# A two-layer diffusion step on one core: modulation products placed singly between filter transform products, gate rows moved inside the transform and ahead of the last row tile

## The chip, the cores and the metric

The kernel runs on one core of one Trainium2 chip. The metric is the device time of one execution in microseconds (us); smaller is better.

## The reference

Two layers work on 1024 sample tokens and 128 prompt tokens of width 1024, all in 32-bit floats. The attention groups and the output projection are untouched by the change. What matters here is the opening of a layer:

```python
mod = silu(c) @ ada_w[i] + ada_b[i]              # (1, 3072), for sample and for context
shift, scale, gate = split(mod, 3)
h = rmsnorm(x, norm_pre) * (1 + scale) + shift
out = mixer(h)                                   # one input projection, four mixers, one output projection
x = x + gate * rmsnorm(out, norm_post)
# one mixer is a Hyena long convolution of order 2: its two filters come from a small
# network times a decay, and are applied through a Fourier transform
spec = rfft(u, 2n) * rfft(filt, 2n); y = irfft(spec)[:n]
```

## The kernel before

The program is written engine by engine. Each engine runs its own list in order; semaphores tie them together. There is no planner: the order in the source is the order on the engine. Token rows are held as nine tiles of 128 (eight of the sample, one of the prompt). All matmul results go to the eight banks of PSUM. `K.next()` hands banks out in turn, so a job takes the bank that the job eight turns earlier had; `claim` makes TensorE wait until that earlier user has been read out (`emptied`), and `done`/`full` tell the reader that a bank is filled.

A layer opens as follows. For filter `o` = 1 and then 0, TensorE makes the nine tiles of the filter (`f3`), which VectorE multiplies by the decay and folds. Then it makes the transform `FE`: turns 0 to 3 (`FE_ORDER`), each with two jobs `p`, and after turn 1 the prompt's job `FEp`. A job of turns 0 and 1 has 4 products of 256 columns, one of turns 2 and 3 has 8, `FEp` has 2. Every 32-bit product shows in the trace as two matmul records and two weight loads, so turns 0 and 1 with `FEp` are 36 records, and turns 2 and 3 are 64.

Six blocks `ada(j)` of the modulation row (silu of the conditioning times a block of 512 columns) stand between these. ScalarE copies each out of its bank (`take_ada`), GpSimd adds the bias (`bias_ada`) and signals `ada_biased`. Block 5 belongs to the gate. In the second filter's transform (`o` = 0):

- TensorE waits for `ada_biased` 3, and turns shift and scale into columns: 16 products (job `modT`), each with a whole 128x128 weight load and only 2 columns. They stand in one block ahead of turn 0. After turn 1 come `FEp` and `ada(5)`, then turns 2 and 3, then the wait for `ada_biased` 5 and the four gate products of 512 columns (`gate_row`), then the transposes of the normalised rows (`x_turned`, L670) and the first input projection, `hyena_input(0, 0)`.
- ScalarE starts on this transform only when the first filter's butterfly and spectrum are finished, since they share buffers. It empties three `FE` banks, then goes on in turns: square of row tile 0, `FE`, square of tile 1, `FEp` (L1381), `take_ada(5)` (L1332), and then again an `FE` bank (L1371) and a square (L1341), up to tile 5.
- VectorE first finishes the butterfly of filter 1 (its last instruction is L1910), and then reads `modT` (L1826, L1827), which frees its bank. It normalises row tiles 0 to 5 (L1772, and L1844 when GpSimd has made the root), multiplies the four gate rows by a norm's gain (`gate_rows`), adds the filter bias (L1897), and then modulates the transposes with ScalarE: VectorE does half of each tile (L1852), ScalarE the other (L1390). `hyena_input(0, 0)` waits until row tiles 0 to 3 are modulated in both halves.
- GpSimd makes the inverse roots of tiles 0 and 1, then `bias_ada(5)`, then the roots of tiles 2 to 5.
- SyncE issues the loads. It stores the gate rows once they are read out of their banks, and loads row tiles 6 to 8 behind that.

Of the kernel before, what the change touches and what calls it, by code (L numbers as in the profile page):

```python
# [37 lines left out]
P = 128  # L38
D = 1024
KD = D // P  # L40
# [95 lines left out]
RING = len(XN)  # L136
# [148 lines left out]
class Banks:  # L285
# [25 lines left out]
    def claim(self, job, banks, drains=1):  # L311

        found = {self.last[b] for b in banks if b in self.last}
        b0 = banks[0]
        self.filled[b0] = self.filled.get(b0, 0) + 1
        self.drains[b0] = self.drains.get(b0, 0) + drains
        for b in banks:
            self.last[b] = (b0, self.drains[b0])
        job = (self.s.layer, job)
        assert job not in self.jobs, job  # L320
        self.jobs[job] = (b0, self.filled[b0], self.drains[b0])
        return [(self.s.raw(f"bank{b}_drained"), v) for b, v in sorted(found)]
# [26 lines left out]
def program(nc, I, outs, known=None):  # L349
    with ExitStack() as ctx:  # L350
        ctx.enter_context(nc.allow_non_contiguous_dma(reason="a few short parameter columns"))
        S = Signals(nc, ctx, known)
        K = Banks(S, known)
# [27 lines left out]
        def at(off, *shape, parts=P, base=0):  # L381

            v = R[base:base + parts, off:off + int(np.prod(shape))]
            if len(shape) == 1:
                return v
            g = "abcd"[:len(shape)]
            return v.rearrange(f"p ({' '.join(g)}) -> p {' '.join(g)}", **dict(zip(g, shape)))

        ident = sb("ident", [P, P])
        sel = sb("sel", [P, 2, P])  # L390
# [268 lines left out]
        def _(pe):  # L659
            def claim(job, banks, drains=1):  # L660
                for w in K.claim(job, banks, drains):
                    pe.wait_ge(*w)
                return bank[banks[0]]

            def mm(out, lhsT, rhs, start=True, stop=True):
                return nc.tensor.matmul(out, lhsT, rhs, start=start, stop=stop)  # L666
# [24 lines left out]
            for l in S.layers():  # L691
# [19 lines left out]


                mod = at(A_MOD, 3072)
                tf = at(TF, 2 * NT, 2, P)
                ti = at(TI, 2 * NT, 2, P)
                eo = at(EO, TT, 3, GW)
                for o in (1, 0):
                    for t in FILTER_ORDER:
                        ps = claim(("f3", o, t), K.next())
                        for h, row0, c, n in (((0, 0, 512, 64), (1, 64, 0, 64)) if t == 4 else  # L720
                                              ((t // 5, 0, t * P - t // 5 * HALF, P),)):
                            last = mm(ps[row0:row0 + n, :], at(F_ARG + c, n, parts=64, base=64 * h),
                                      at(A_FW3 + o * 512, 512, parts=64, base=64 * h))
                        last.then_inc(*K.done(("f3", o, t)))
                    ada(0 if o else 4)
                    if o:
                        pe.wait_ge(*S.at("transform_table"))
                    else:
                        if l == 0:
                            pe.wait_ge(S.raw("constants"), 16 * N_CONST)  # L730
                        pe.wait_ge(*S.at("ada_biased", 3))
                        ps = claim(("modT",), K.next())
                        for m in range(2 * KD):
                            last = mm(ps[:, 2 * m:2 * m + 2], mod[:, m * P:(m + 1) * P], sel[:, :, 0])
                        last.then_inc(*K.done(("modT",)))

                    for turn, a0 in enumerate(FE_ORDER):
                        back = (4 - a0) % 4
                        if a0 % 2:
                            pe.wait_ge(*K.emptied(("f3", o, 7)))  # L740
                            pe.wait_ge(*S.at("filter_negated", o))
                        else:
                            pe.wait_ge(*S.at("filter_folded", (o, a0 + 4)))
                        if o and turn % 2:
                            ada((turn + 1) // 2)
                        if o == 0 and turn == 2:
                            ada(5)
                        for p in range(2):
                            ps = claim(("FE", o, a0, p), K.next())
                            for ri in range(2):  # L750
                                if a0 % 2:
                                    terms = [(a, 0) for a in (a0, a0 + 4)] + [(a, 1 + ri) for a in (back, back + 4)]
                                else:
                                    terms = [(a, 2 * ri) for a in (a0, a0 + 4)]
                                for i, (a, kind) in enumerate(terms):
                                    last = mm(ps[:, ri * GW:(ri + 1) * GW], tf[:, 2 * a + p, ri, :],
                                              eo[:, a, kind, :], i == 0, i == len(terms) - 1)
                            last.then_inc(*K.done(("FE", o, a0, p)))
                        if turn == 1:
                            pe.wait_ge(*S.at("filter_folded", (o, NT)))  # L760
                            ps = claim(("FEp", o), K.next())
                            for ri in range(2):
                                last = mm(ps[:, ri * GW:(ri + 1) * GW], tf[:, 0, ri, :], eo[:, NT, 2 * ri, :])
                            last.then_inc(*K.done(("FEp", o)))
                    if o:
                        ada(3)
                    else:
                        pe.wait_ge(*S.at("ada_biased", 5))
                        for s in range(2):
                            for half in range(2):  # L770
                                ps = claim(("gate_row", s, half), K.next())
                                mm(ps[:, :], sel[:, s, :], mod[:, 2 * D + half * 512:2 * D + (half + 1) * 512]
                                   ).then_inc(*K.done(("gate_row", s, half)))

                def x_turned(t, banks):
                    pe.wait_ge(*S.at("x_normed", t))
# [93 lines left out]
                for o in range(2):  # L870
                    for a0 in (0, 2, 1, 3):
# [4 lines left out]
                        for p in range(2):  # L876
                            ps = claim(("Z", o, a0, p), K.next())
                            for ri in range(2):
                                for i, a in enumerate((a0, a0 + 4)):
                                    last = mm(ps[:, ri * GW:(ri + 1) * GW], tf[:, 2 * a + p, ri, :],  # L880
                                              zv[:, a, 2, :], i == 0, i == 1)
# [368 lines left out]
                for grp in ("gqa", "diff0", "diff1"):  # L1250
# [3 lines left out]
                    for i in range(1, TT + 1):  # L1254
# [3 lines left out]
                        t = i + AHEAD[grp] - 1  # L1258
# [501 lines left out]
        def _(v):  # L1760
# [49 lines left out]
            for l in S.layers():  # L1810
# [20 lines left out]
                def gate_rows():  # L1831

                    for s in range(2):
                        for half in range(2):
                            job = ("gate_row", s, half)
                            v.wait_ge(*K.full(job))
                            tt(at(SGH + s * D + half * 512, 512), B(job), at(A_NPOST + half * 512, 512), ALU.mult
                               ).then_inc(*K.drained(job))
# [45 lines left out]
                for o in (1, 0):  # L1884
                    if o == 0:
                        modulation()
                        for t in range(RING):
                            normalize(t)
                        gate_rows()

                    for a0 in range(4):
                        for p in range(2):
                            v.wait_ge(*K.emptied(("FE", o, a0, p)))
                    E = at(B2, 4, 2, 2, GW)
                    bias = at(A_HBIAS[o], GW)
                    for p in range(2):
                        link(nc.vector.scalar_tensor_tensor(E[:, 0, p, 0, :], bias, 1.0 / N_SAMPLE, E[:, 0, p, 0, :],  # L1897
                                                            ALU.mult, ALU.add), "bias_added", (o, p))
                    if o == 0:
                        v.wait_ge(*K.emptied(("gate_row", 1, 1)))  # L1900
                        for t in range(TT):
                            modulate(t)
                            if t >= 4 and t + 2 < TT:
                                normalize(t + 2)
                        v.wait_ge(*S.at("spectrum1_kept"))
                    butterfly(("F", o), B2, B3, HS, -1)
                    v.wait_ge(*K.emptied(("FEp", o)))
                    nc.vector.scalar_tensor_tensor(at(HS + 4096, GW), bias, 1.0 / N_PROMPT, at(B2 + 4096, GW),
                                                   ALU.mult, ALU.add)
                    nc.vector.tensor_copy(at(HS + 4096 + GW, GW), at(B2 + 4096 + GW, GW)  # L1910
                                          ).then_inc(*S.up(f"spectrum{o}_made"))
# [687 lines left out]
```

## Time and profile before

| | before |
|---|---|
| median of 3 runs (lowest, highest) | 2400.47 us (2398.37, 2400.97) |
| profiled execution, its own time | 2400.11 us |
| its span, first to last instruction | 2398.3 us |
| TensorE busy | 2247.9 us, 94% |
| VectorE busy | 1292.0 us, 54% |
| ScalarE busy | 943.5 us, 39% |
| GpSimd busy | 307.9 us, 13% |
| mean granted TensorE clock | 0.990 |

PE is TensorE's matmuls, PEld its weight loads, DVE VectorE, ACT ScalarE, POOL GpSimd, SP SyncE. A clock of 1.00 is 2.4 GHz, and 0.50 is 1.2 GHz. Line numbers are those of the kernel before; L666 and L670 are the helpers that record every matmul and every transpose, L1767 and L2369 those of VectorE's and GpSimd's two-operand instructions.

### The profile page before, as it was taken

How to read it: one execution, taken by the hardware profiler on the slowest of the kernel's cores; microseconds unless marked ns; L12 is line 12 of the kernel's file. 1: busy time of each engine (PE TensorE's matmuls, PEld its weight loads, DVE VectorE, ACT ScalarE, POOL GpSimd, SP SyncE). 2: the span in 40 equal slices, each digit the busy share in tenths (PEclk: the TensorE clock that was granted, in tenths of full speed). 3: DMA queues.
4: the chain of work that ended last, by engine and by line, in shares of the span. 5: the costliest groups of instructions: out<-in, count | busy, mean ns of one | idle time of the engine just before them, and what ended most of it. 6: DMA issues, size and time to landing. Idle time of an engine off the chain costs nothing. (4 is left out here: it accounts for less than half of the span.)

```text
span 2398.3 us, 36438 instructions
## 1 busy us (share of the span) xinstructions
PE 2247.9 (94%) x14536; PEld 1586.7 (66%) x14536; DVE 1292.0 (54%) x2418; ACT 943.5 (39%) x1939; POOL 307.9 (13%) x458
## 2 busy tenths in 40 slices
PE   6999999899999998989999999999999999889898
PEld 4656865685567776864866577657854777768657
DVE  3642764564656465583546247555545654855732
ACT  2422113553255265483224221135521652745721
POOL 0410001000100013022324000010011000220323
PEclk9999999999999999999999999999999999999999
DMA  7600100100010000113276001001001100002022
GB/s 237 247 36 29 57 18 1 55 2 15 17 63 2 4 5 7 37 37 133 79 255 224 29 1 57 19 17 39 1 15 38 42 1 8 1 7 72 2 88 88
DMA packets 75039, 124.93 MB, mean 52 GB/s; under 512 B 25778, under 2 KB 38962, under 8 KB 73332
## 3 DMA queue, kind: packets, MB, share of 16 engines
q1 hardware_dynamic: 73816, 121.64, 14.7%
q8 instruction: 117, 1.92, 0.3%
q10 hardware_dynamic: 1056, 0.96, 0.2%
q14 instruction: 50, 0.41, 0.1%
HBM read 105.38 MB, written 17.20 MB: 51 GB/s over the span
## 5 line engine op out<-in xcount | busy, mean ns | idle before, releaser
L666 PE MATMUL psum<-arena 128*32 128x128 f32 (+9 forms) x9392 | 1483.4, 389 | 54.2 <-ACT arena L1322 11.9
L666 PEld LDWEIGHTS psum<-arena 128*32 128x32 f32 (+3 forms) x9392 | 921.6, 150 | 541.6 <-issue 408.1
L670 PE MATMUL psum<-ident,arena 128*128 128x128 f32 (+1 forms) x2248 | 333.4, 278 | 67.7 <-ACT arena L1586 31.4
L1767 DVE TENSOR_TENSOR arena<-arena 128x32 f32<-128x32 f32 (+10 forms) x686 | 307.7, 494 | 111.3 <-ACT arena L1462 42.6
L670 PEld LDWEIGHTS psum<-ident,arena 128*128 128x128 f32 (+1 forms) x2248 | 251.6, 140 | 153.8 <-issue 103.5
L666 PE MATMUL psum<-k_parts,q_parts 96*128 96x384 f32 (+2 forms) x1000 | 267.3, 362 | 17.2 <-ACT arena L1497 6.0
L2061 DVE TENSOR_REDUCE st<-psum 128x1 f32<-128x1152 f32 (+1 forms) x144 | 177.9, 1236 | 52.4 <-PE psum L666 52.1
L2156 DVE TENSOR_REDUCE st<-psum 128x1 f32<-128x1152 f32 (+1 forms) x144 | 174.6, 1236 | 51.9 <-PE psum L666 51.4
L666 PEld LDWEIGHTS psum<-k_parts,q_parts 96*128 96x128 f32 (+1 forms) x1000 | 168.4, 190 | 35.3 <-issue 16.9
L1497 ACT ACTIVATE arena<-psum,st 128x1152 f32<-128x1152 f32 (+1 forms) x144 | 162.5, 1128 | 51.0 <-DVE st L2061 43.5
L1767 DVE TENSOR_TENSOR arena<-psum,arena 128x512 f32<-128x512 f32 (+2 forms) x104 | 57.1, 564 | 227.6 <-PE psum L666 227.6
L1512 ACT COPY arena<-psum 128x512 f32<-128x512 f32 (+1 forms) x244 | 102.1, 434 | 185.9 <-PE psum L670 185.8
L1572 ACT ACTIVATE arena<-psum,st 128x1152 f32<-128x1152 f32 (+1 forms) x144 | 162.4, 1129 | 27.7 <-DVE st L2156 26.8
L2369 POOL TENSOR_TENSOR arena<-arena 128x512 f32<-128x512 f32 (+4 forms) x74 | 135.8, 1847 | 192.7 <-ACT arena L1332 82.8
L2369 POOL TENSOR_TENSOR st<-st,minus 128x1 f32<-128x1 f32 x72 | 42.9, 596 | 740.1 <-ACT arena L1572 740.1
L2075 DVE COPY arena<-psum 128x512 f32<-128x512 f32 (+1 forms) x156 | 93.5, 612 | 28.9 <-PE psum L670 28.9
L1586 ACT COPY arena<-psum 128x512 f32<-128x512 f32 (+1 forms) x200 | 90.3, 470 | 43.3 <-PE psum L670 42.5
L2166 DVE SCALAR_TENSOR_TENSOR arena<-arena,st 128x1152 f32<-128x1152 f32 (+1 forms) x72 | 96.0, 1333 | 11.7 <-POOL st L2369 11.7
L1928 DVE SCALAR_TENSOR_TENSOR arena<-arena,hcw 128x1024 f32<-128x1024 f32 x24 | 30.8, 1285 | 125.9 <-ACT arena L1416 125.5
L1535 ACT ACTIVATE arena<-psum 128x512 f32<-128x512 f32 x36 | 21.5, 598 | 172.0 <-PE psum L666 172.0
L2369 POOL TENSOR_TENSOR st<-st,mhalf 128x1 f32<-128x1 f32 (+2 forms) x72 | 56.3, 782 | 243.5 <-DVE st L1772 243.4
L1696 ACT CAST q_parts<-psum 96x512 fp32r<-96x512 f32 (+1 forms) x54 | 31.7, 588 | 117.1 <-PE psum L670 116.5
(149 smaller groups left out, 1704.4 us busy)
## 6 DMA issues: line engine op xcount, KB each, us to landing
arena<-in_ada_w SPq DMA_DIRECT2D x12, 2048.0 KB, 9.1
arena<-in_w_in SPq DMA_DIRECT2D x10, 2048.0 KB, 8.8
arena<-in_x SPq DMA_DIRECT2D x18, 512.0 KB, 5.7
out_xs<-arena SPq DMA_DIRECT2D x18, 512.0 KB, 2.6
arena<-out_xs SPq DMA_DIRECT2D x18, 512.0 KB, 5.7
arena<-in_w_out SPq DMA_DIRECT2D x4, 2048.0 KB, 7.8
spectrum_kept<-arena SPq DMA_DIRECT2D x2, 2304.0 KB, 8.4
arena<-spectrum_kept SPq DMA_DIRECT2D x2, 2304.0 KB, 8.9
```

What stands on the lines that cost most here:

```text
L666: return nc.tensor.matmul(out, lhsT, rhs, start=start, stop=stop)
L670: return nc.tensor.transpose(out, src, ident[0:n, 0:n])
L1497: nc.scalar.activation(at(buf, nk, w), psum[:, 512 * b0:512 * (b0 + nk)].rearrange("p (c n) -> p c n", c=nk)[:, :, 0:w], ACT.Exp, bias=st[ ...
L1512: nc.scalar.copy(at(SLOTS[grp] + slot(grp, u) * 1152 + 512 * j, nk * P), bank[b][:, 0:nk * P]).then_inc(*S.up("turned_scalar", (grp, number)))
L1572: nc.scalar.activation(at(buf, nk, w), psum[:, 512 * b0:512 * (b0 + nk)].rearrange("p (c n) -> p c n", c=nk)[:, :, 0:w], ACT.Exp, bias=st[ ...
L1586: nc.scalar.copy(at(SLOTS[grp] + slot(grp, u) * 1152 + 512 * j, nk * P), bank[b][:, 0:nk * P]).then_inc(*S.up("turned_scalar", (grp, number)))
L1767: return nc.vector.tensor_tensor(out, a, b, op)
L2061: nc.vector.tensor_reduce(st[:, 16 + x % 4:17 + x % 4], psum[:, 512 * b0:512 * (b0 + nk)].rearrange("p (c n) -> p c n", c=nk)[:, :, 0:w], ...
L2075: nc.vector.tensor_copy(at(SLOTS[grp] + slot(grp, u) * 1152 + 512 * j, nk * P), bank[b][:, 0:nk * P]).then_inc(*S.up("turned_vector", (grp ...
L2156: nc.vector.tensor_reduce(st[:, 16 + x % 4:17 + x % 4], psum[:, 512 * b0:512 * (b0 + nk)].rearrange("p (c n) -> p c n", c=nk)[:, :, 0:w], ...
L2166: nc.vector.scalar_tensor_tensor(p0, p1, c, p0, ALU.mult, ALU.add).then_inc(*S.up("mixed", (grp, u)))
L2369: return nc.gpsimd.tensor_tensor(out, a, b, op)
```

## The change

The block of 16 modulation products is dissolved. Its bank is still claimed at the same place, ahead of turn 0, and the wait for `ada_biased` 3 stays there. Each product now stands behind one of the 16 wide products of turns 0 and 1. The four gate products, with their wait for `ada_biased` 5, move from behind turn 3 to between turns 2 and 3. On VectorE the reading of the gate rows moves from behind the normalisation of row tile 5 to behind that of tile 4. Nothing is computed otherwise, and the lists of ScalarE, GpSimd and SyncE stay as they are.

```diff
+                def modulation_column(m, columns):
+                    last = mm(columns[:, 2 * m:2 * m + 2], mod[:, m * P:(m + 1) * P], sel[:, :, 0])
+                    if m == 2 * KD - 1:
+                        last.then_inc(*K.done(("modT",)))
...
                         pe.wait_ge(*S.at("ada_biased", 3))
-                        ps = claim(("modT",), K.next())
-                        for m in range(2 * KD):
-                            last = mm(ps[:, 2 * m:2 * m + 2], mod[:, m * P:(m + 1) * P], sel[:, :, 0])
-                        last.then_inc(*K.done(("modT",)))
+                        columns = claim(("modT",), K.next())
...
                                     last = mm(ps[:, ri * GW:(ri + 1) * GW], tf[:, 2 * a + p, ri, :],
                                               eo[:, a, kind, :], i == 0, i == len(terms) - 1)
+                                    if o == 0 and turn < 2 and (ri, i) != (1, len(terms) - 1):
+                                        modulation_column(8 * turn + 4 * p + 2 * ri + i, columns)
                             last.then_inc(*K.done(("FE", o, a0, p)))
+                            if o == 0 and turn < 2:
+                                modulation_column(8 * turn + 4 * p + 3, columns)
...
+                        if o == 0 and turn == 2:
+                            pe.wait_ge(*S.at("ada_biased", 5))
+                            for s in range(2):
+                                for half in range(2):
+                                    ps = claim(("gate_row", s, half), K.next())
+                                    mm(ps[:, :], sel[:, s, :], mod[:, 2 * D + half * 512:2 * D + (half + 1) * 512]
+                                       ).then_inc(*K.done(("gate_row", s, half)))
                     if o:
                         ada(3)
-                    else:
-                        pe.wait_ge(*S.at("ada_biased", 5))
...
                         for t in range(RING):
                             normalize(t)
-                        gate_rows()
+                            if t == RING - 2:
+                                gate_rows()
```

## Rows read from the trace of the kernel before

**Rows 1.** Waits of PE between 60 and 232 us: total, times, longest.

```profile
PE psum L666 <- DVE arena L1852: 4.2, 2, 3.4
```

**Rows 2.** Timeline of PE, layer 1: start, length, instructions, idle before and releaser.

```profile
70.17 5.00 PE L666 MATMUL psum<-sel,arena 128*128 128x2 f32 x32
75.03 25.93 PE L666 MATMUL psum<-arena 128*128 128x256 f32 x116
100.81 3.60 PE L666 MATMUL psum<-arena,sel 128*128 128x512 f32 x8
104.24 3.66 PE L670 MATMUL psum<-ident,arena 128*128 128x128 f32 x32
...
112.90 8.80 PE L666 MATMUL psum<-arena 128*128 128x512 f32 x16 [3.37 <-DVE arena L1852]
...
123.29 7.03 PE L666 MATMUL psum<-arena 128*128 128x512 f32 x16
```

**Rows 3.** Windows (start:end, length, busy by engine; PEclk is the fourth last).

```profile
72.38:79.20 6.82, 6.82 (x24) 6.01 (x24) 6.72 (x8) 1.67 (x4) 3.51 (x1) 0.50 0.51 169
...
86.89:100.81 13.92, 13.92 (x69) 12.27 (x66) 5.90 (x14) 9.79 (x19) 8.09 (x9) 1.00 0.78 288
113.34:116.75 3.41, 3.41 (x5) 1.35 (x4) 2.42 (x4) 3.24 (x8) 1.78 (x2) 0.50 0.43 175
...
1250.29:1253.39 3.10, 3.10 (x32) 3.10 (x28) 2.92 (x7) 0.88 (x2) 0.00 (x0) 1.00 0.02 5
1253.39:1260.21 6.82, 6.82 (x20) 5.65 (x20) 6.72 (x7) 1.37 (x4) 4.40 (x1) 0.50 0.63 214
```

**Rows 4.** Timeline of ACT, layer 1.

```profile
88.38 1.57 ACT L1371 ACTIVATE arena<-psum 128x512 f32<-128x512 f32 x3 [13.20 <-DVE arena L1910]
...
92.86 0.61 ACT L1332 COPY arena<-psum 128x512 f32<-128x512 f32 x1
...
101.50 1.05 ACT L1341 ACTIVATE arena<-arena 128x1024 f32<-128x1024 f32 x1
```

**Rows 5.** Timeline of DVE, layer 1.

```profile
88.21 0.16 DVE L1827 SCALAR_TENSOR_TENSOR mcol<-psum,gpre 128x16 f32<-128x16 f32 x1
...
100.04 0.75 DVE L1844 TENSOR_SCALAR arena<-arena,st 128x1024 f32<-128x1024 f32 x1 [0.66 <-POOL st L2369]
...
103.49 0.75 DVE L1844 TENSOR_SCALAR arena<-arena,st 128x1024 f32<-128x1024 f32 x1 [0.67 <-POOL st L2369]
104.16 2.48 DVE L1767 TENSOR_TENSOR arena<-psum,arena 128x512 f32<-128x512 f32 x4
106.55 0.87 DVE L1897 SCALAR_TENSOR_TENSOR arena<-arena 128x256 f32<-128x256 f32 x2
107.46 6.47 DVE L1852 TENSOR_SCALAR arena<-psum,mcol 128x128 f32<-128x128 f32 x20
```

**Rows 6.** Timeline of POOL: bias of block 5 in layer 1 and layer 2.

```profile
93.61 1.62 POOL L2369 TENSOR_TENSOR arena<-arena 2x512 f32<-2x512 f32 x1 [0.28 <-ACT arena L1332]
...
1273.72 1.62 POOL L2369 TENSOR_TENSOR arena<-arena 2x512 f32<-2x512 f32 x1 [0.29 <-ACT arena L1332]
```

**Rows 7.** Timeline of PE, layer 2: end of the transform and first projection.

```profile
1254.35 26.77 PE L666 MATMUL psum<-arena 128*128 128x256 f32 x116
1280.96 3.60 PE L666 MATMUL psum<-arena,sel 128*128 128x512 f32 x8
...
1293.05 8.80 PE L666 MATMUL psum<-arena 128*128 128x512 f32 x16 [2.44 <-DVE arena L1852]
```

**Rows 8.** Timeline of PE at two other waits, one in each layer.

```profile
268.93 3.26 PE L666 MATMUL psum<-arena 128*128 128x256 f32 x14 [3.61 <-issue]
...
1453.65 2.65 PE L666 MATMUL psum<-arena 128*128 128x256 f32 x8 [3.61 <-issue]
```

**Rows 9.** Windows behind those two waits, columns as in group 3.

```profile
268.93:272.30 3.37, 3.37 (x16) 2.98 (x17) 3.37 (x7) 0.77 (x3) 0.00 (x0) 1.00 0.00 0
...
1454.80:1458.20 3.40, 3.40 (x9) 2.70 (x8) 3.16 (x7) 1.01 (x3) 0.00 (x0) 0.50 0.00 0
```

More of the change, by code:

```diff
@@ L764, in _ @@
                             last.then_inc(*K.done(("FEp", o)))
+                        if o == 0 and turn == 2:
[5 more added lines that the diff above has]
+                                       ).then_inc(*K.done(("gate_row", s, half)))
                     if o:
                         ada(3)
-                    else:
-                        pe.wait_ge(*S.at("ada_biased", 5))
[L769 to L773, printed above, removed]
                 def x_turned(t, banks):
```

## Prediction

> **What bounds the kernel now.** I began with the page's busy shares: TensorE is busy for 94% of the span, so time is won or lost where TensorE waits, or where it runs slowly. The waits of TensorE in the first layer's opening come next [rows 1]: the only large one is 3.4 us, for VectorE's modulation (L1852), just ahead of the first input projection. The reader should see that until then TensorE arrives in time for everything. The timeline of TensorE places the parts [rows 2]: narrow block at 70.17, transform from 75.03, gate products at 100.81, transposes at 104.24, projection at 112.90. The windows give the clock [rows 3]: from 72.38 to 79.20 it is at 0.50, that is 1.2 GHz. TensorE was doing the narrow products when it fell, and wide products had followed when it rose. Layer 2 has the same at 1253.39 to 1260.21. Last I read the lists of ACT, DVE and POOL over the same stretch [rows 4 to 6], because TensorE's new waits are for them, and here is the surprise: ScalarE begins on this transform only at 88.38, when VectorE has finished the other filter.
>
> **Part 1: the modulation products.** As a block at the full clock: in layer 2, 3.10 us at 1.00, then 0.96 us (1253.39 to 1254.35 [rows 3, 7]) at 0.50, worth 0.48: 3.58 us for 32 records, 0.112 each. A wide record takes 13.92 / 64 = 0.2175 us [rows 3]. Standing singly, a narrow product's first load can hide under the wide product ahead of it; its second load, and that of the wide product behind it, cannot, since 2 columns cover nothing. That is two exposed loads for each product, as in the block. I take the same 3.58 us. Bounds: 0 if all hides; half as much again, 5.4 us, if three loads are exposed.
>
> What the singles do give back is the clock. It fell while narrow products followed each other; now a wide product stands ahead of each, and behind wide products alone the rows show 1.00 [rows 3], so I expect no fall here. 6.82 us at half rate become 3.41 us. So TensorE is 3.41 us early behind turn 1 and `ada(5)`: turn 2 starts at 86.89 - 3.41 = 83.48.
>
> **Part 2: the first new wait, a bank.** From `modT` the turns run: modT, FE, FE, FE, FE, FEp, ada 5, FE (turn 2, p 0), FE (turn 2, p 1). The last is eight turns behind modT and takes its bank. VectorE frees it at 88.21 + 0.16 = 88.37 [rows 5]. Before, TensorE asked for it at 86.89 + 3.48 = 90.37, 2.0 us behind. Now it asks at 83.48 + 3.48 = 86.96, and waits 1.4 us. VectorE cannot be earlier: it comes from the butterfly, which no edit touches. The job then ends at 88.4 + 0.1 + 3.48 = 92.0.
>
> **Part 3: the second new wait, the bias of block 5.** The gate products now stand here, and need `ada_biased` 5. ScalarE copies block 5 at 92.86 only [rows 4], at the end of a list without gaps that began at 88.38 with the butterfly; GpSimd adds the bias from 93.61 to 95.23 [rows 6]. At the old place (100.81) this was 5.6 us early. At the new place TensorE stands from 92.0 to about 95.3, 3.3 us, and turn 3 is queued behind it: nothing else that TensorE could do is let past. Even without any clock gain TensorE would arrive at 93.8, ahead of the bias. So the gain of part 1 is swallowed whole, and its bounds do not matter: with 0 or 5.4 us for the narrow products, or with a clock that falls all the same, TensorE still comes before 95.2.
>
> Then four gate products, 104.24 - 100.81 = 3.43 us, with 0.2 for the first exposed load, to 98.9; turn 3 is half of 13.92, 6.96 us. Call the end of the transform and gate products T. Before, the transform ended at T = 100.81 and the gate products stood behind it; after, T = 105.8, 5.0 us later.
>
> **Part 4: the tail.** Before, from T = 100.81 [rows 4, 5]: ScalarE's square of tile 5 starts at T+0.7, VectorE scales the tile at T+2.7 to T+3.4, reads the gate rows to T+5.8, adds the filter bias, and modulates from T+6.65. The sixteenth of its 20 modulations (0.32 each, 5.2 us, and 0.2 until TensorE starts) lets the projection go at T+12.09 [rows 2]. After: VectorE is done with tile 4 at about T-0.0 (100.79 before), reads the gate rows until T+2.4, while the square of tile 5 runs. Tile 5 is next: its variance on VectorE and root on GpSimd take 0.8 us ahead of the scaling (0.67 of it the idle in the row), so the scaling starts at T+3.2 instead of T+2.7 and ends at T+3.9, the filter bias takes 0.87, modulation from T+4.75, projection at T+10.2. The move gives 1.9 us. Bounds: 0 if something else is late, and 2.48 if all four reads hide. The transposes start at T instead of T+3.43; some must wait for banks that the gate rows hold until T+2.4, but with 3.7 us of work they are done by T+6.1, ahead of a modulation that runs until T+11. ScalarE's half, 5.7 us, can start at T+2.45, and is not last. SyncE stores the gate rows at T+2.5 = 108.3 instead of 106.7, and the loads of tiles 6 to 8 follow it; they are needed behind the projection, 7 us later, and have slack.
>
> Sum for layer 1: +5.0 - 1.9 = +3.1 us: the projection starts at 116.0 instead of 112.9. From there to the end of the stage TensorE has no wait over 1 us [rows 1], so the delay goes on to the end. Layer 2 has the same distances: bias at 1273.72 + 1.62 = 1275.34, T at 1280.96, projection 12.09 behind it [rows 6, 7]. Two layers: +6.2 us.
>
> **Part 5: the clock behind the new wait.** The wait of 3.3 us may lower the clock while gate products and turn 3 run, now on the path. A wait of 3.37 us at 109.5 was followed by 0.50 from 113.34 to 116.75 [rows 2, 3]; one of 2.44 by a projection as slow, 8.80 instead of 7.03 us [rows 2, 7]; of two of 3.61 us one was followed by 0.50 and one not [rows 8, 9]. Three of four. A fall costs 8.80 - 7.03 = 1.77 us, so for two layers 2 x 0.75 x 1.77 = 2.7 us, between 0 and 3.5. The later fall, behind the wait for the modulation, stays, since that wait stays.
>
> The Trainium skill (TensorE: Matmul & The Clock Gate, section "HAM oscillation — how this bites in real kernels") lets every burst that follows such a wait start at the half rate. By that rule both layers fall, and the sum would be +9.7 us instead of +8.9; the trace agrees in three of four waits, and I go by the rows.
>
> Sum: 6.2 + 2.7 = 8.9 us. The profiled execution took 2400.11 us (span 2398.3, 1.8 around it), which gives 2409.0; it lies 0.4 below the median of the runs, so I forecast 2409.3 us, 0.37% slower. Changes under 0.2%, about 4.8 us, count as none.
>
> **The rivals.**
> - *The clock's gain arrives (faster).* No wait takes over; the place is the two waits of parts 2 and 3. Then TensorE saves 3.41 us and the tail 1.9, twice: 2400.5 - 10.6 = 2389.9. For it: the low clock is there, the move on VectorE is real. Against it: the bias must be signalled by 90.5 instead of 95.2, and modT's bank be freed by 87.0, though VectorE's filter work ends at 88.2. Chance 0.08.
> - *Break-even.* Only the wait for the bank binds, since block 5 comes sooner than I think; it decides once the bias lands at about 92.1. Then T = 92.0 + 3.6 + 7.0 = 102.6, +1.8 - 1.9 = -0.1 a layer, no change. With a bias at 94, half way, it is +1.8 a layer, 2404.1, just within 0.2%. Against it: ScalarE's list is dense. Chance 0.10.
> - *Worse than forecast.* The 1.4 us and 3.3 us waits together, 3.5 us apart, keep the clock low for twice as long, as at 72.38, or VectorE's 1.9 us do not appear: 2400.5 + 6.2 + 2 x 3.4 = 2413.5, or 2413.1. Chance 0.10.
> - *The forecast*: both waits bind in both layers, with none, one or two falls: 2406.7, 2408.4 or 2410.2. Chance 0.72.
>
> **Range.** From 2403.5, where the break-even cases end, to 2412.5. Faster 0.08, same 0.10, slower 0.82.
>
> **What would show it.** In the timeline of PE: no row of 32 narrow records, clock 1.00 from 70 to 87; then an idle of about 1.4 us ahead of the second job of turn 2, released by DVE (L1827 before), and one of about 3.3 us ahead of the gate products, released by POOL. Gate products at 95.3, transposes from about 105.8, projection at 116.0. On DVE the gate rows start at about 105.7, followed by a scaling, and the modulation at 110.5. ScalarE's first `FE` copy stays at 88.4. I am wrong if that start moves, if the bias comes before 94, or if the loss of the opening is made up behind 116.

## The result, and the profile after

| | before | after |
|---|---|---|
| median (lowest, highest), 6 runs each | 2399.28 us (2398.37, 2400.97) | 2409.12 us (2407.78, 2412.99) |
| profiled execution, its own time | 2400.11 us | 2412.99 us |
| its span | 2398.3 us | 2411.2 us |

The ratio is 1.0042, with a 95% interval from 1.0029 to 1.0055: the change is 9.8 us slower. The forecast was 2409.3 us, slower. The profiled execution is the slowest of the six, 3.9 us above their median, so its places and waits are to be read, and its total is not.

The timeline of PE in layer 1, for [rows 2]:

```profile
79.44 0.28 PE L666 MATMUL psum<-sel,arena 128*128 128x2 f32 x2
79.58 0.68 PE L666 MATMUL psum<-arena 128*128 128x256 f32 x2
...
80.23 6.62 PE L666 MATMUL psum<-arena 128*128 128x256 f32 x36
87.98 3.72 PE L666 MATMUL psum<-arena 128*128 128x256 f32 x16 [1.13 <-DVE mcol L1835]
94.84 5.40 PE L666 MATMUL psum<-arena,sel 128*128 128x512 f32 x8 [3.14 <-POOL arena L2378]
100.08 7.07 PE L666 MATMUL psum<-arena 128*128 128x256 f32 x32
106.98 4.73 PE L670 MATMUL psum<-ident,arena 128*128 128x128 f32 x36
113.08 0.66 PE L670 MATMUL psum<-ident,arena 128*128 128x128 f32 x4 [1.37 <-DVE arena L1860]
117.11 9.88 PE L666 MATMUL psum<-arena 128*128 128x512 f32 x16 [3.37 <-DVE arena L1860]
```

The block of 32 narrow records is gone; pairs of narrow and of wide records alternate. Two waits are new ahead of the transposes, and both name their cause: 1.13 us for VectorE's reading of the modulation columns, which frees the bank, and 3.14 us for GpSimd's bias. A third, 1.37 us in the transposes, costs nothing: behind it TensorE still waits 3.37 us for the modulation. The transposes start at 106.98, where the transform before had ended at 100.81, and the projection at 117.11 instead of 112.90. Layer 2, for [rows 7]:

```profile
1276.35 3.72 PE L666 MATMUL psum<-arena 128*128 128x256 f32 x16 [1.12 <-DVE mcol L1835]
1283.20 5.39 PE L666 MATMUL psum<-arena,sel 128*128 128x512 f32 x8 [3.13 <-POOL arena L2378]
...
1297.86 4.56 PE L670 MATMUL psum<-ident,arena 128*128 128x128 f32 x40 [2.35 <-DVE arena L1775]
1305.46 7.11 PE L666 MATMUL psum<-arena 128*128 128x512 f32 x16 [3.04 <-DVE arena L1860]
```

The same two waits to 0.01 us. Ahead of the transposes TensorE waits 2.35 us here (1.18 before) for VectorE to empty the gate rows' banks; this too lies ahead of the wait for the modulation and costs nothing.

How much did an opening lose? I call opening the time from TensorE's first record of the second filter's transform to the first projection. Before, that first record is a narrow one, at 70.17. After, it is the first wide product, which the view puts into one row with the filter products ahead of it; record by record it starts at 69.73 in layer 1 and 1258.11 in layer 2, 0.54 us ahead of the first narrow row. So the opening takes 117.11 - 69.73 = 47.4 us in layer 1 and 1305.46 - 1258.11 = 47.3 in layer 2, where it was 42.7 and 42.8. Each opening lost 4.6 us.

The windows, for [rows 3]:

```profile
70.27:87.98 17.71, 16.58 (x99) 13.22 (x98) 17.34 (x17) 1.90 (x6) 12.64 (x5) 1.00 0.47 179
95.39:98.80 3.41, 3.41 (x6) 1.35 (x5) 1.61 (x3) 0.69 (x2) 0.55 (x1) 0.50 0.76 295
...
272.88:279.70 6.82, 5.49 (x13) 4.39 (x14) 6.46 (x14) 1.81 (x5) 0.00 (x0) 0.50 0.00 0
```

The clock held at 1.00 over the spread products. It stands at 0.50 behind the new wait, under the gate products. The last row is luck of this execution: at the wait of 3.6 us behind which the trace before went on at full clock [rows 8, 9], the clock stood at 0.50 for 6.82 us here. TensorE was busy for 5.49 of them, so about 2.7 us were lost.

ScalarE's copy of block 5 and GpSimd's bias, for [rows 4, 6]:

```profile
92.42 0.61 ACT L1340 COPY arena<-psum 128x512 f32<-128x512 f32 x1
```

```profile
93.17 1.62 POOL L2378 TENSOR_TENSOR arena<-arena 2x512 f32<-2x512 f32 x1 [0.28 <-ACT arena L1340]
```

The bias is there at 94.79; TensorE goes at 94.84. VectorE, for [rows 5]:

```profile
106.88 2.48 DVE L1775 TENSOR_TENSOR arena<-psum,arena 128x512 f32<-128x512 f32 x4
...
110.08 0.75 DVE L1852 TENSOR_SCALAR arena<-arena,st 128x1024 f32<-128x1024 f32 x1 [0.66 <-POOL st L2378]
110.75 0.88 DVE L1906 SCALAR_TENSOR_TENSOR arena<-arena 128x256 f32<-128x256 f32 x2
111.66 6.47 DVE L1860 TENSOR_SCALAR arena<-psum,mcol 128x128 f32<-128x128 f32 x20
```

The gate rows are read ahead of tile 5, and the modulation starts 4.68 us behind the end of the transform, where it was 6.65.

### The profile page after: what moved, and what is told of

It reads as the page before. It is cut to its first block and busy times, and to the rows that moved or that the text cites. A ratio compares the mean times of both kernels' runs of the same rounds, so it can differ in the third digit from the quotient of the medians.

```text
span 2411.2 us, 36438 instructions
## 1 busy us (share of the span) xinstructions
PE 2250.3 (93%) x14536; PEld 1588.9 (66%) x14536; DVE 1291.0 (54%) x2418; ACT 942.8 (39%) x1939; POOL 307.0 (13%) x458
## 5 line engine op out<-in xcount | busy, mean ns | idle before, releaser
L1505 ACT ACTIVATE arena<-psum,st 128x1152 f32<-128x1152 f32 (+1 forms) x144 | 162.4, 1128 | 51.0 <-DVE st L2070 42.8
L2175 DVE SCALAR_TENSOR_TENSOR arena<-arena,st 128x1152 f32<-128x1152 f32 (+1 forms) x72 | 96.0, 1333 | 11.6 <-POOL st L2378 11.6
```

The costliest lines, as they stand in the source:

```text
L1505: nc.scalar.activation(at(buf, nk, w), psum[:, 512 * b0:512 * (b0 + nk)].rearrange("p (c n) -> p c n", c=nk)[:, :, 0:w], ACT.Exp, bias=st[ ...
L2175: nc.vector.scalar_tensor_tensor(p0, p1, c, p0, ALU.mult, ALU.add).then_inc(*S.up("mixed", (grp, u)))
```

## The experiments

Each of these runs was measured beside the kernel before; the ratios are to that. The theory: the loss is the wait of the gate products for the bias of block 5, and the low clock behind it; the clock's gain over the narrow products is swallowed by the waits. The main rival: one of the pieces is bad in itself, the singles or the place between turns 2 and 3.

**e1: the modulation products alone.** The gate products and `gate_rows()` go back to their old places.

```diff
-                        if o == 0 and turn == 2:
-                            pe.wait_ge(*S.at("ada_biased", 5))
...
                     if o:
                         ada(3)
+                    else:
+                        pe.wait_ge(*S.at("ada_biased", 5))
...
...
-                            if t == RING - 2:
-                                gate_rows()
+                        gate_rows()
```

> Only the modulation products are spread; the gate products and their reading stay where they were before. Theory A (the loss comes from the gate products' wait for the bias of block 5, and the clock's gain is limited only by the bank that VectorE frees at 87.9): an idle of about 1.2 us ahead of the second job of turn 2, none ahead of the gate products, transform ended at 98.6 instead of 100.8, projection at 110.7: 2.1 us gained a layer, about 2395 us. Rival B (the bank's wait does not bind, the whole 3.4 us a layer arrives): 2392.5 us. Rival C (the singles themselves cost what the clock gives back): 2399 us or more.

Measured: 2398.25 us (11 runs), ratio 0.9996 (0.9987 to 1.0005). The timeline of PE is as theory A has it:

```profile
87.89 10.63 PE L666 MATMUL psum<-arena 128*128 128x256 f32 x48 [1.12 <-DVE mcol L1835]
98.35 3.60 PE L666 MATMUL psum<-arena,sel 128*128 128x512 f32 x8
```

The wait for the bank is there, and none ahead of the gate products. The opening takes 40.8 us in both layers, 1.9 and 2.0 less than in the first trace of before. The singles are not to blame for the loss. But of the 3.9 us that this should bring, 1.0 arrived, within what cannot be told from none; by the time alone rival C (2399 us) is closer than theory A (2395). e8 shows why.

**e2: the gate products alone.** The other half: the modulation block as before, gate products and their reading moved as in the change.

> Only the gate products and their reading are moved; the modulation products stay one block, with the low clock behind them. Theory A: TensorE comes to the gate products at 93.8 and waits 1.0 to 1.4 us for the bias; the transform ends at 105.5 instead of 100.8, VectorE's reorder gives 1.9 back, projection at 115.6: 2.7 us lost a layer, and no fall of the clock behind so short a wait: about 2404.7 us, some 4 below the changed kernel. Rival C (the singles are to blame for the loss, the move is a gain of 1.9 a layer): 2395.5 us.

Measured: 2408.47 us (5 runs), ratio 1.0040 (1.0027 to 1.0052). So the move alone makes the whole loss. The size was missed by 3.8 us:

```profile
94.74 3.70 PE L666 MATMUL psum<-arena,sel 128*128 128x512 f32 x8 [2.87 <-POOL arena L2370]
```

I expected a wait of at most 1.4 us, counting on the long fall of the clock over the block. In this trace the block took 3.85 us (before: 5.00), so TensorE came sooner and waited the rest. In layer 2 it waited 2.85 us, and there the gate products ran at half rate besides, 5.36 us instead of 3.70: behind nearly the same wait the clock fell in one layer and not in the other.

**e3: the bias made early, in the changed kernel.**

```diff
                         negate((1, 5, 3, 7))
+                        take_ada(5)
...
-                        if o == 0 and turn == 2:
-                            take_ada(5)
...
                     if o == 0:
+                        bias_ada(5)
                         for t in range(RING):
                             inverse_root(("x", t), st[:, t:t + 1])
-                            if t == 1:
-                                bias_ada(5)
```

> The changed kernel with block 5 copied by ScalarE ahead of its wait for the butterfly, and its bias added by GpSimd ahead of the inverse roots. Theory A: the bias is there at about 91.5, the idle of 3.1 us ahead of the gate products is gone or under 0.3 us, the idle for the bank stays; the transform ends at about 102, projection at 112.2: level with the kernel before or up to 1 us better a layer, about 2398 us, some 11 below the changed kernel. Rival D (the place of the gate products between turns 2 and 3 costs by itself, whatever they wait for): above 2404 us.

Measured: 2399.16 us (11 runs), ratio 1.0000 (0.9991 to 1.0009), 10.0 below the changed kernel. The timeline of PE:

```profile
87.88 3.72 PE L666 MATMUL psum<-arena 128*128 128x256 f32 x16 [1.13 <-DVE mcol L1834]
91.44 3.67 PE L666 MATMUL psum<-arena,sel 128*128 128x512 f32 x8
94.95 7.07 PE L666 MATMUL psum<-arena 128*128 128x256 f32 x32
101.85 4.73 PE L670 MATMUL psum<-ident,arena 128*128 128x128 f32 x36
```

With the bias ready, the wait of 3.14 us is gone, and the fall of the clock behind it, 1.7 us: 4.9 a layer, 9.7 for both, of the 10.0 measured. Rival D's time (above 2404 us) is refuted. But the place is not free. The four gate products now stand ahead of turn 3 and hold it up by 3.5 us, of which VectorE's reorder gives 2.0 back: the opening takes 42.3 and 42.4 us here and 40.8 in e1, 1.5 us a layer more. The medians of the two runs are 0.9 us apart. The loss is gone against the kernel before, since what the spread products gain against its low clock about pays for the place.

**e4: VectorE reads the gate rows last, in the changed kernel.**

```diff
-                            if t == RING - 2:
-                                gate_rows()
+                        gate_rows()
```

> The changed kernel with VectorE's reading of the gate rows put back behind the normalisation of tile 5. Theory A: both of TensorE's new waits stay, and the modulation starts 1.9 us later a layer: 2413 us, 3.8 above the changed kernel. Rival E (the reading is hidden either way): 2409 us.

Measured: 2412.79 us (5 runs), ratio 1.0058 (1.0046 to 1.0071), 3.7 above the changed kernel. VectorE's reorder is a gain, 1.9 us a layer, as worked out. In layer 1, from the end of the transform (106.80) to the modulation (113.45) it is again 6.65 us. In layer 2 the opening grows by 4.0 us, since the transposes wait 5.81 us for the banks and then run partly at half rate.

```profile
110.14 2.48 DVE L1775 TENSOR_TENSOR arena<-psum,arena 128x512 f32<-128x512 f32 x4
112.54 0.87 DVE L1905 SCALAR_TENSOR_TENSOR arena<-arena 128x256 f32<-128x256 f32 x2
113.45 6.47 DVE L1860 TENSOR_SCALAR arena<-psum,mcol 128x128 f32<-128x128 f32 x20
```

**e5: the bank freed early, in the changed kernel.**

```diff
                     if o == 0:
-                        modulation()
                         for t in range(RING):
...
                     butterfly(("F", o), B2, B3, HS, -1)
+                    if o:
+                        modulation()
                     v.wait_ge(*K.emptied(("FEp", o)))
```

> The changed kernel with VectorE's reading of the modulation columns put ahead of the last two instructions of the first filter's spectrum, so that the bank is free some 2.7 us sooner. Theory A: the idle of 1.1 us ahead of the second job of turn 2 goes, and the idle ahead of the gate products, whose bias comes when it came, grows from 3.1 to about 4.3 us: no gain, 2409 us. Rival B (the bank's wait carries part of the loss): 2.2 us less, 2407 us.

Measured: 2410.36 us (5 runs), ratio 1.0045 (1.0031 to 1.0060). The timeline of PE:

```profile
94.76 6.40 PE L666 MATMUL psum<-arena,sel 128*128 128x512 f32 x8 [4.56 <-POOL arena L2379]
```

The first wait moved into the second, 4.56 us in place of 1.13 and 3.14, and nothing was gained. Waits in a row on one engine don't add up as causes: where the last one's signal does not hang on the earlier ones, it alone sets the time.

**e6: e1 with that early bank.**

> Spread modulation products, gate products at their old place, and the bank freed early as in e5. Theory A: with no wait behind it the earlier bank is a gain of 1.1 us a layer: transform ended at 97.2, projection at 109.3, about 2396 us, 2 below the run with singles only. Rival F (VectorE or ScalarE then bounds the opening): no gain, 2398 us.

Measured: 2393.54 us (12 runs), ratio 0.9976 (0.9966 to 0.9986): this version is faster than both kernels. The timeline of PE:

```profile
97.61 3.60 PE L666 MATMUL psum<-arena,sel 128*128 128x512 f32 x8
...
109.96 8.80 PE L666 MATMUL psum<-arena 128*128 128x512 f32 x16 [3.36 <-DVE arena L1860]
```

The direction is theory A's. The size is not settled: the median is 4.7 us below e1, and the openings, 39.7 us instead of 40.8, explain 2.3 us. The runs of e6 go from 2389.9 to 2398.7 us and those of e1 from 2395.6 to 2400.2, and the low clock elsewhere differs from one execution to the next by as much.

**e7: two more moves in the tail.** On top of e6:

```diff
+                            if o == 0 and 2 * turn + p == 7:
+                                square(5)
                             act.wait_ge(*K.full(job))
...
                         for t in range(RING):
                             normalize(t)
+                            if t == 1:
+                                filter_bias()
```

> As e6, and two more moves in the tail: ScalarE squares row tile 5 ahead of the last transform copy, and VectorE adds the filter bias behind the normalisation of tile 1 instead of ahead of the modulation. Theory A: the tail is VectorE's list; 0.87 us of filter bias leave it, and tile 5 is normalised before TensorE has the gate rows: modulation from about 103, projection at about 108.5, 4.4 us sooner than before a layer and 0.9 sooner than e6: about 2394.5 us. Rival F: as e6, no further gain.

Measured: 2402.88 us (11 runs), ratio 1.0015 (1.0006 to 1.0023): slower, and neither theory foresaw it. VectorE and then GpSimd in layer 1:

```profile
100.76 4.99 DVE L1854 TENSOR_SCALAR arena<-arena,st 128x1024 f32<-128x1024 f32 x1 [0.66 <-POOL st L2389]
```

```profile
100.17 0.55 POOL L2389 TENSOR_TENSOR st<-st,mhalf 128x1 f32<-128x1 f32 x1 [0.93 <-DVE st L1782]
100.69 4.51 POOL L2389 TENSOR_TENSOR arena<-arena 128x2048 f32<-128x2048 f32 x1
```

With the filter bias added early, nothing kept GpSimd from its butterfly, which it began at 100.69. VectorE's scaling of tile 5, 0.75 us in the kernel before, took 4.99 (4.98 in layer 2) and ended 0.55 us behind it.

**e9: e7 without the early filter bias.**

> e7 without its early filter bias: spread modulation products, early bank, tile 5 squared ahead of the last transform copy. Theory G (e7 lost because the early bias let GpSimd's butterfly of 4.51 us start while VectorE still had tile 5 to scale, and that scaling took 4.99 us instead of 0.75): the scaling is back at 0.75 us, projection at about 109.5, 2393 us, as e6 or up to 1 us better. Rival H (the early square cost e7 its time): 2402 us.

Measured: 2394.55 us (11 runs), ratio 0.9986 (0.9977 to 0.9995). The scaling of tile 5 on VectorE:

```profile
99.87 0.75 DVE L1854 TENSOR_SCALAR arena<-arena,st 128x1024 f32<-128x1024 f32 x1 [0.66 <-POOL st L2380]
```

Theory G holds: taking the early filter bias out gives back 8.3 us, and the one blocked instruction a layer accounts for 8.5. The early square brings nothing that the runs can tell: the opening takes 39.6 us, in e6 39.7.

**e8: the kernel before, one more trace.**

> The kernel before, for one more trace. If the length of the low clock behind the block of narrow products differs from execution to execution, it is 3.41 us in one or both layers here instead of 6.83, and the transform ends up to 1.7 us sooner; this would explain why taking the block apart gives less on average (1.0 us) than the first trace promised (4.9 us). If it is 6.83 in both layers again, that explanation falls.

Measured: 2399.77 us, one run. The timeline of PE in layer 1, for [rows 2]:

```profile
69.97 3.73 PE L666 MATMUL psum<-sel,arena 128*128 128x2 f32 x32
73.56 13.52 PE L666 MATMUL psum<-arena 128*128 128x256 f32 x68
88.21 10.63 PE L666 MATMUL psum<-arena 128*128 128x256 f32 x48 [1.13 <-DVE mcol L1827]
98.68 3.60 PE L666 MATMUL psum<-arena,sel 128*128 128x512 f32 x8
```

In layer 1 the clock did not fall at all over the same block. TensorE came early to the bank and waited 1.13 us, exactly as it does with the products spread. From the transform's start to that job TensorE took 88.21 - 1.13 - 69.97 = 17.1 us, as in the changed kernel (86.85 - 69.73), so spreading the products costs nothing; in the first trace it took 20.3. Two windows of the same trace, in layer 2:

```profile
1253.80:1256.30 2.50, 2.50 (x21) 2.42 (x21) 2.50 (x5) 1.22 (x3) 0.00 (x0) 1.00 0.02 7
1256.40:1259.70 3.30, 3.30 (x10) 2.56 (x9) 3.20 (x5) 0.42 (x1) 2.26 (x1) 0.50 0.56 180
```

There it fell for half as long as in the first trace. The openings take 40.8 and 41.1 us, e1's 40.8. So the low clock that the spread products do away with is worth 0 to 2.0 us a layer, whichever the execution brings; the first trace happened to show the most. This explains e1 and the miss of e2. Nor is the whole execution shorter by what an opening saves: e8's two openings are 3.6 us shorter than the first trace's, its time is 0.3 us shorter. Its clock stood low at other places instead, one of them around the end of the first wait of [rows 8], where the first trace kept 1.00:

```profile
266.51:273.34 6.83, 5.47 (x13) 4.43 (x14) 6.47 (x14) 1.81 (x5) 0.00 (x0) 0.50 0.00 0
```

**e11: the changed kernel, one more trace.**

> The changed kernel once more, for a second trace. The two waits of TensorE (1.1 and 3.1 us in each layer) are the same; the low clock behind the second lies elsewhere or is absent, and the time falls with it towards the median of 2409 us. If the low clock stands in the same places with the same length, it does not vary and the rest of the first trace's 4 us above the median is unexplained.

Measured: 2411.26 us, one run. The timeline of PE and a window:

```profile
94.77 6.70 PE L666 MATMUL psum<-arena,sel 128*128 128x512 f32 x8 [3.15 <-POOL arena L2378]
```

```profile
94.00:100.82 6.82, 6.05 (x7) 2.52 (x8) 1.76 (x4) 2.00 (x5) 1.81 (x3) 0.50 1.02 356
```

The wait is the same to 0.01 us; the low clock around its end is twice as long as in the first trace. In four openings of two traces it was there every time.

**e10: the changed order with everything early.** The change, e5's early bank, block 5 copied as in e3 but its bias added within GpSimd's butterfly, tiles 4 and 5 squared ahead of turn 3's copies, and the gate rows read one by one in VectorE's idle:

```diff
                     nc.vector.tensor_scalar(st[:, t:t + 1], st[:, t:t + 1], 1.0 / D, EPS, ALU.mult, ALU.add
                                             ).then_inc(*S.up("variance", ("x", t)))
+                    if 2 <= t < RING:
+                        gate_row(t - 2)
                     v.wait_ge(*S.at("inverse_root", ("x", t)))
```

> The changed order on TensorE (modulation products spread, gate products between turns 2 and 3) with what it waited for made early: block 5 copied and its bias added before ScalarE's first transform copy, the modulation columns read early, each gate row read by VectorE while it waits for GpSimd's root of tiles 2 to 5, tiles 4 and 5 squared ahead of turn 3's copies. Theory A (the place between turns 2 and 3 is good once nothing is late there): no idle on TensorE before the transposes, transform ended at about 100.6, modulation from 101.5, projection at about 107: some 5 us a layer ahead of the kernel before, 2388 us. Rival D (the place costs by itself): above 2394 us. Rival F (another wait takes over in the tail): 2391 to 2394 us, with the wait to be seen ahead of the projection.

Measured: 2395.74 us (11 runs), ratio 0.9981 (0.9973 to 0.9990). Of the three, rival F is nearest in kind, since another wait takes over, but none has it all: the time lies 1.7 us above F's range and within rival D's, and the new wait is not where F put it. The timeline of PE, layer 1 and then layer 2:

```profile
90.04 3.60 PE L666 MATMUL psum<-arena,sel 128*128 128x512 f32 x8
93.47 7.07 PE L666 MATMUL psum<-arena 128*128 128x256 f32 x32
100.38 4.53 PE L670 MATMUL psum<-ident,arena 128*128 128x128 f32 x40
107.68 8.64 PE L666 MATMUL psum<-arena 128*128 128x512 f32 x16 [2.77 <-DVE arena L1865]
...
1297.44 1.10 PE L670 MATMUL psum<-ident,arena 128*128 128x128 f32 x8 [2.59 <-DVE arena L1857]
```

The projection of layer 1 is 5.2 us ahead of [rows 2], nearly as expected, and no wait stands before the transposes. The opening takes 38.0 us in both layers, 1.6 less than in e9. In layer 2 a new wait of 2.59 us stands ahead of the transposes of tile 6, whose load is late. The page of transfers from 1270 to 1300 us, and one row of that of the kernel before, from 1268:

```profile
arena<-in_w_in SPq DMA_DIRECT2D x2, 2048.0 KB, 16.1
...
arena<-out_xs SPq DMA_DIRECT2D x3, 512.0 KB, 13.2
```

```profile
arena<-out_xs SPq DMA_DIRECT2D x3, 512.0 KB, 8.0
```

Tiles 6 to 8 are issued from 1280.6, where it was 1287.2, and take 13.2 us to land instead of 8.0: issued 6.6 us sooner behind the same weights, they land about 1.4 us sooner. In layer 2 of this trace the transfers bound the opening.

The median shows little of it: e10 is no faster than e9 (2394.55 us), which has the gate products at their old place. What became of the shorter openings beyond the wait for tile 6 I have not settled.

**e12: the second projection ahead of the transposes of tile 6.**

```diff
-                x_turned(6, ([6], [7]))
                 hyena_input(1, 0, [3])
+                x_turned(6, ([6], [7]))
```

> e10 with the second input projection, hyena_input(1, 0), ahead of the transposes of tile 6 on TensorE. In e10's layer 2 row tile 6 lands only at 1293.5 behind 9.2 MB of other transfers, and TensorE waits 2.6 us for its transposes. Theory A: that wait is covered by the 7 us projection, everything else as in e10: 2.6 us less, about 2393 us, and 2391 us where the wait's low clock goes too. Rival F: the wait only moves behind the projection, since the transfers land later still: 2395.7 us.

Measured: 2402.31 us (12 runs), ratio 1.0015 (1.0006 to 1.0024). The timeline of PE in layer 1:

```profile
128.03 1.97 PE L670 MATMUL psum<-ident,arena 128*128 128x128 f32 x8 [3.06 <-DVE arena L1857]
```

A miss for theory A, and in a way that rival F did not say either. VectorE modulates tile 6 ahead of normalising tile 8; with the transposes of tile 6 later, VectorE waits 2.38 us for them, tile 8 is late, and TensorE waits 3.06 us for it, now in both layers.

**The openings side by side**, from one trace of each run, in us:

| run | layer 1 | layer 2 | median of the runs |
|---|---|---|---|
| before (first trace, e8) | 42.7, 40.8 | 42.8, 41.1 | 2399.28 |
| changed (first trace, e11) | 47.4, 48.7 | 47.3, 47.1 | 2409.12 |
| e1, singles only | 40.8 | 40.8 | 2398.25 |
| e2, gate products only | 45.7 | 47.3 | 2408.47 |
| e3, bias early | 42.3 | 42.4 | 2399.16 |
| e4, rows read last | 49.2 | 51.3 | 2412.79 |
| e5, bank early | 48.4 | 47.3 | 2410.36 |
| e6, e1 with early bank | 39.7 | 39.7 | 2393.54 |
| e7, e6 with two moves | 44.6 | 45.2 | 2402.88 |
| e9, e6 with one of them | 39.6 | 39.6 | 2394.55 |
| e10, all early | 38.0 | 38.0 | 2395.74 |
| e12, e10 reordered | 38.0 | 38.1 | 2402.31 |

e10 and e12 lose time behind the point at which the opening ends here.

## Why the prediction was right

- **Part 1, the narrow products.** Forecast 0.112 us a record, the same singly: a pair and its wide neighbours take 79.58 to 80.23, 0.65 us, and 2 x 0.2175 of it is the wide product, so 0.22 for two narrow records. Right. The clock held: right. But the 3.41 us a layer that I set for it is too much and not steady. Up to the second job of turn 2 TensorE took 20.3 us in the first trace and 17.1 in e8's layer 1, so the long fall cost 3.2 us; e8 shows no fall in one layer and half of it in the other. This reached my expectations of e1 and e2, and it also reaches the sum: that counts from T = 100.81, a time with the long fall in it. Against e8 the changed kernel's first trace lost 6.6 and 6.3 us in its openings, not 4.6.
- **Part 2, the bank.** Forecast 1.4 us, measured 1.13. The whole transform started 0.44 us sooner in this execution, at 69.73. From there VectorE freed the bank after 18.19 us, in both kernels; TensorE asked for it after 17.12 and not, as forecast, 16.8, which is the overrated fall of part 1. That ScalarE's first `FE` copy stands at 87.94 and not at 88.4, which I had called a sign of being wrong, is the same shift: 18.21 us behind the start in both. e5 shows that this wait costs nothing by itself.
- **Part 3, the bias.** Forecast 3.3 us, measured 3.14, released by GpSimd. e3 takes it away, and with it the loss against the kernel before.
- **Part 4, the tail.** Forecast: modulation from T+4.75, projection at T+10.2; measured 111.66 - 106.98 = 4.68 and 117.11 - 106.98 = 10.13. e4 confirms the 1.9 us a layer.
- **Part 5, the clock behind the wait.** Forecast three of four, 1.77 us each. Measured four of four in two traces. Gate products and turn 3 took 106.98 - 94.84 = 12.14 us; at full clock, in e3, 101.85 - 91.44 = 10.41: 1.73 us for one fall. In e11 the fall is longer, 108.21 - 94.77 = 13.44, 3.03 us. The term was 2.7 us for both layers and should have been 3.5 or more. By the rule of the Trainium skill that I weighed there (TensorE: Matmul & The Clock Gate, section "HAM oscillation — how this bites in real kernels"), every burst behind such a wait starts at the half rate; the four openings agree. Other waits do not: the first wait of [rows 8], 3.61 us, is followed by 1.00. The last sentence of part 5, that the later fall stays, held in layer 1 alone, where the projection took 9.88 us (8.80 before); in layer 2, behind a wait of 3.04 us, it took 7.11 (8.80), and the same two are 8.56 and 7.10 in e11.
- **The sum.** 3.1 us a layer without falls; with one fall 4.9, against 4.6 measured in each opening. Medians: 9.8 us of loss against 8.9 forecast. The mechanism is shown from both sides (e2 has the loss without the singles, e3 has the change without the loss). That the number is so close is in part luck, for the first trace of before had the long fall in both layers. Over two traces of each kernel the two openings together take 83.7 us before and 95.3 after, 11.6 more; the two projections behind them took 18.1 and 16.3, 1.8 less. The difference is 9.8, as the medians have it, but from four traces that agreement may itself be luck. How the falls further on, such as that at 272.88, are spread over executions is not settled.

The rivals: the gain did not arrive, as both waits bound. Break-even came true only once its condition, an early bias, was made true, in e3.

## What to carry to other kernels

Ahead of moving work forward on an engine that is full, look up when each of its inputs is signalled, not whether the wait was free at the old place: here a signal 5.6 us early became one 3.1 us late, and all that stood behind it in the queue paid. When a wait is removed and another is next in the same queue, nothing is won until the last one goes. Ask also what stands behind the moved work: even with the bias early the gate products held up turn 3, and the opening of e3 is 1.5 us longer than that of e1. Only e10, with the reads hidden as well, has a shorter opening than its counterpart e9, and no shorter time; in layer 2 its next bound was a transfer. One trace is not enough to price a low clock: take it from two executions before building on it.

## What the runs showed of the hardware

- The same 32 narrow records ran wholly at 1.00 in one execution (e8, layer 1) and ended at 0.50 in another [rows 2, 3]; over six passages (the first trace, e2 and e8) the low clock behind them lasted 6.83, 6.83, 3.41, 3.41, 0 and 3.41 us. With a 256-column product ahead of each narrow one the clock stayed at 1.00 in all 22 passages of eleven traces. A narrow record came every 0.112 us at 1.00 and every 0.213 us at 0.50 (before, 70.30 to 72.31 and 72.47 to 74.82). Executions of the kernel before spread over 2395 to 2407 us.
- A VectorE scaling of 128x1024 in SBUF took 4.99 us instead of 0.75 beside a GpSimd two-operand instruction of 4.51 us that had started 0.07 us ahead, and ended 0.55 us behind its end (e7). The Trainium skill (SBUF — State Buffer, section "Who interferes with whom") says that the two share a pair of ports, that a VectorE scaling can enter a mode which needs that pair, and that then the one issued first blocks the other for its whole instruction; this trace agrees. VectorE's modulation, which reads PSUM, kept its 0.32 us [rows 5] beside the same kind of butterfly in the kernel before:

```profile
107.68 4.52 POOL L2369 TENSOR_TENSOR arena<-arena 128x2048 f32<-128x2048 f32 x1 [4.22 <-DVE arena L1897]
```

- GpSimd's bias of 2x512 took 1.62 us where VectorE scaled a tile at the same time [rows 6], and 1.26 us elsewhere in that trace (at 63.50, for one); in e3, where no scaling ran beside it, the bias of block 5 took 1.25.
